# A two-layer diffusion backbone with expert retrieval: plain fp32 products while selecting, three-pass products only at the end

## The chip, the cores and the metric

The kernel runs on one core of a Trainium2 chip. The metric is the device time of one execution in microseconds; the median of three runs stands for a kernel. PE is TensorE, DVE is VectorE, ACT is ScalarE, POOL is GpSimd, SP the engine that issues most DMAs.

## What is computed

640 tokens (512 latent, 128 context) of width 1024 go through two layers. Each layer mixes tokens and then retrieves experts:

```python
def peer_ffn(h, wq, sub_keys, u_tab, v_tab):
    q = (x @ wq).reshape(n, PEER_HEADS, 2, PEER_DQ // 2)
    s = jnp.einsum('nhcd,hckd->nhck', q, sub_keys)
    s1, i1 = lax.top_k(s[:, :, 0], 16); s2, i2 = lax.top_k(s[:, :, 1], 16)
    cand = s1[..., :, None] + s2[..., None, :]
    top, pos = lax.top_k(cand, 16)          # per head, of 8 heads
    idx = take_along_axis(i1 * 128 + i2, pos); gate = softmax(top)
    act = gelu(einsum('nd,nhkd->nhk', x, u_tab[idx]))
    return einsum('nhk,nhkd->nd', gate * act, v_tab[idx])
```

`u_tab` and `v_tab` have 16384 rows of 1024 numbers in each layer.

## The kernel before

The program is written out engine by engine, with semaphores; no scheduler moves anything. A layer is a loop iteration (`nc.Fori(0, DEPTH)` in `build`) of stages; this case is about its second half.

Three of the five token tiles of 128 are computed densely: the hidden values of **all** 16384 experts are formed for the 384 tokens (ND), multiplied with a gate that is zero nearly everywhere, and multiplied with all of V. The other two tiles (SPARSE = 2) fetch only their own rows: 128 rows of U and 128 of V per token, gathered by POOL, one row for each of 128 tokens at a time.

U is treated in 128 blocks of 128 experts. A block is a load of 512 KB (`HiddenAhead.load`, on SP), a rounded high part (`u_high`, ACT, L1469), the low part that is left (`u_low`, DVE, L1473), and on PE eight times `split3`: low x high, high x low, high x high (L196 to L198) on fp32r operands, 384 columns each, into a PSUM bank. ACT then takes the GELU (L1491). Raw blocks, high and low parts each have two slots. The first 64 blocks (AHEAD) are done in the stages before the experts and stored to DRAM (`spill`):

- **Query** (`gemm(g, "query", ...)`): the second normalization (`norm_programs`) writes h as a high and a low part, g.h2; then the queries.
- **Selection** (`select_stage`): for each of five tiles, PE forms 16 score matrices (L1569, plain fp32, 128 x 128), DVE finds the top 16 of each, combines and selects (L1633 to L1717), ACT takes an exponent (L1617), PE turns the result (L1578). Blocks 0 to 51 of U are placed by hand between these steps: `PER_TILE = 11` blocks to a tile, with positions p at which PE turns the last tile's result (p == 1) and forms the next scores (p == 3), and at which ACT takes the exponent (p == 5); `low(t, p)` places the low parts in DVE's list.
- **Gates** (`gates_stage`): 12 turns with two half-tiles each. DVE makes one-hot matrices (L1782, L1783, L1788), PE multiplies them (L1805, 48 bf16 matmuls), half a U block follows on PE, ACT copies the gates out (L1831), SP stores them. Blocks 52 to 63.
- **Experts** (`experts_stage`): 32 turns. A turn takes four blocks of V (high part L1997, low part L2042), two spilled and two new hidden blocks, and weighs them with the gates (L2051, L2056). Between these steps DVE handles 16 gathered rows: in turns 0 to 15 a dot product of a U row with h of the token (L2065), tile 0 first and then tile 1; in turns 16 to 31 a multiply-add of a V row to the token's sum (L2074), again tile by tile, so that each row adds to the sum that the row before it wrote:

```python
r = gathered(i, q)
ve.wait_ge(used, i * PER_TURN + q)
ve.scalar_tensor_tensor(acc[:, x, :], r, w, acc[:, x, :], ALU.mult, ALU.add).then_inc(used, 1)
```

  The rows lie in a ring of 8 slots that POOL fills (L1912). At the start PE turns h of the two tiles into token order (L1965), after the gates have been stored (`stores_done`).

The order of work is set by these lists alone. SP's list holds loads and spills in order; POOL's holds the gathers.

Of the kernel before, what the change touches and what calls it, by code (L numbers as in the profile page):

```python
# [434 lines left out]
def norm_programs(g, st, name, out, gain, shift, low=None):  # L435
# [6 lines left out]
    sq = g.sb(st, "sq", [P, 2, NT])  # L442
    rs = g.sb(st, "rs", [P, 2, NT])
    t = g.sb(st, "t", [P, 3, NT])
    raw = (lambda kc: out[:, kc, :]) if low is None else (lambda kc: t[:, kc % 3, :])
# [30 lines left out]
    def vector(ve):  # L476
# [9 lines left out]
        for kc in range(KC):  # L486
            if low is not None and kc >= 3:
# [947 lines left out]
PER_TILE = 11  # L1435
IN_SELECT = 52
SPARSE = 2
# [4 lines left out]
class HiddenAhead:  # L1442
# [5 lines left out]

    def __init__(self, g, st, l):
        self.g, self.l = g, l  # L1450
        self.u = g.sb(st, "u", [P, 2, KC, P])
        self.u2 = [g.sb(st, f"u{x}", [P, 2, KC, P], F32R) for x in ("hi", "lo")]
        self.hh = g.sb(st, "hh", [P, 2, ND])
        self.u_in = [g.sem(f"u_loaded{i}") for i in range(2)]
        self.spilled = [g.sem(f"hidden_stored{i}") for i in range(2)]
        self.u_hi, self.u_lo, self.h_ready, self.h_taken = (g.sem(f"exp_{x}") for x in ("u_high", "u_low", "h_ready", "h_taken"))
# [7 lines left out]
    def u_high(self, act, n, slot, times, first=False):  # L1464

        act.wait_ge(self.u_in[slot], times * 16)
        if not first:
            act.wait_ge(self.h_ready, n - 1)
        self.g.nc.scalar.activation(self.u2[0][:, slot, :, :], self.u[:, slot, :, :], ACT.Copy).then_inc(self.u_hi, 1)  # L1469

    def u_low(self, ve, n, slot):
        ve.wait_ge(self.u_hi, n + 1)
        ve.tensor_tensor(self.u2[1][:, slot, :, :], self.u[:, slot, :, :], self.u2[0][:, slot, :, :].bitcast(F32),  # L1473
                         ALU.subtract).then_inc(self.u_lo, 1)

    def products(self, pe, slot, chunks):
# [6 lines left out]
    def hidden(self, pe, n, slot, first=False):  # L1483
        pe.wait_ge(self.u_lo, n + 1)
        if not first:
            pe.wait_ge(self.h_taken, n - 1)
        self.products(pe, slot, range(KC)).then_inc(self.h_ready, 1)
# [16 lines left out]
class Gathered:  # L1504
# [4 lines left out]
    def __init__(self, g, st):  # L1509
        self.rows = [g.sb(st, "rows", [P, P], U32) for _ in range(SPARSE)]  # L1510
        self.share = [g.sb(st, "share", [P, P]) for _ in range(SPARSE)]
        self.act = [g.sb(st, "act", [P, P]) for _ in range(SPARSE)]

    def row_numbers(self, ve, k, x, first, second, base):

        k.then(ve.scalar_tensor_tensor(self.act[x][:, :], first, float(NKEY), second, ALU.mult, ALU.add))
        k.did(ve.tensor_scalar(self.rows[x][:, :], self.act[x][:, :], base, None, ALU.add))


def select_stage(g, l, qT, sel, kt, loaded, hid, own):  # L1520
# [10 lines left out]
    lists = g.sem("sel_lists_done")  # L1531
    NC = 2 * PH
    TAIL = P - TOPK // 2
    with ExitStack() as st, nc.Block() as block:
# [17 lines left out]
        def blocks(t):  # L1552
            return [(n - t * PER_TILE, n) for n in range(t * PER_TILE, min((t + 1) * PER_TILE, IN_SELECT))]

        @block.sync
        def _(sync):
            for n in range(IN_SELECT):
                hid.load(sync, n + 2, n % 2)
# [3 lines left out]
        def _(pe):  # L1562
# [17 lines left out]

            pe.wait_ge(loaded, 16)
# [11 lines left out]
        def _(act):  # L1593
# [10 lines left out]
            hid.u_high(act, 0, 0, 1, first=True)  # L1604
            hid.u_high(act, 1, 1, 1, first=True)
            scores(0)
            for t in range(TILES):
                for p, n in blocks(t):
                    hid.u_high(act, n + 2, n % 2, n // 2 + 2)
                    hid.gelu_to_spill(act, n, n % 2, n // 2, first=n < 2)  # L1610
                    if p == 1 and t >= 1:
                        selected(t - 1)
                    if p == 3 and t + 1 < TILES:
                        scores(t + 1)
                    if p == 5:
# [5 lines left out]
        def _(ve):  # L1621
            k = Counter(ve, steps)

            def low(t, p):

                for q, n in blocks(t):
                    if q == p:
                        hid.u_low(ve, n + 2, n % 2)

            def top16(n, values, scratch, best, index, t, replaced, found):  # L1630
# [4 lines left out]
                for i in range(n):  # L1635
                    k.did(ve.match_replace(scratch[:, i, :], best[:, i, 0:8], values[:, i, :], NEG))
                    k.did(ve.max_index(index[:, i, 0:8], best[:, i, 0:8], values[:, i, :]))
                    if i in replaced:
                        low(t, replaced[i])
# [4 lines left out]
                for i in range(n):  # L1644
                    k.did(ve.max_index(index[:, i, 8:16], best[:, i, 8:16], scratch[:, i, :]))
                    if i in found:
                        low(t, found[i])
                k.wait()

            hid.u_low(ve, 0, 0)  # L1650
            hid.u_low(ve, 1, 1)
# [3 lines left out]
            for t in range(TILES):  # L1655
                ve.wait_ge(sc_taken, t + 1)
                top16(NC, s, s2, v16, i16, t, {3: 0, 13: 1}, {3: 2})
# [12 lines left out]
                low(t, 3)  # L1670
                k.wait()
                top16(PH, cand, c2, top, pos, t, {5: 4}, {})
                low(t, 5)
# [24 lines left out]
                low(t, 6)  # L1698
# [4 lines left out]

# [3 lines left out]
                for c in range(2):  # L1707
                    k.did(ve.tensor_reduce(res[:, c, :, :], oh[:, c, :, :, :].rearrange("p m k h -> p h k m"), AX.X, ALU.add))
                    if c == 0:
                        low(t, 7)  # L1710
# [7 lines left out]
                low(t, 8)  # L1718
                low(t, 9)
                low(t, 10)  # L1720
# [12 lines left out]
def gates_stage(g, l, sel, hid, store, own):  # L1733
# [8 lines left out]
    with ExitStack() as st, nc.Block() as block:  # L1742
# [9 lines left out]
        def turns(eng, body):  # L1752

            with eng.Fori(0, TG // 2 - 1) as i:
                for q in range(2):
# [642 lines left out]
```

## Time and profile before

| | |
|---|---|
| median of 3 runs | 5162.43 us (5157.72 to 5165.9) |
| profiled execution | 5158.91 us, its span 5157.1 us |
| PE busy | 4192.3 us, 81%; mean granted clock 0.891 |
| DVE busy | 3765.5 us, 73% |
| ACT busy | 1603.1 us, 31% |
| POOL busy | 1497.4 us, 29% |
| DMA | 1079 MB, 209 GB/s over the span |
| selection, gates, experts of layer 0 | 1072 to 1395, to 1560, to 2574 us |

A busy share is an average over stages with different limits. What counts is read stage by stage: which engine is full there, and what the others wait for. Starts of successive instructions tell what one really takes from its engine; the printed duration includes latency that overlaps the next one.

### The profile page before, as it was taken

How to read it: one execution, taken by the hardware profiler on the slowest of the kernel's cores; microseconds unless marked ns; L12 is line 12 of the kernel's file. 1: busy time of each engine (PE TensorE's matmuls, PEld its weight loads, DVE VectorE, ACT ScalarE, POOL GpSimd, SP SyncE). 2: the span in 40 equal slices, each digit the busy share in tenths (PEclk: the TensorE clock that was granted, in tenths of full speed). 3: DMA queues.
4: the chain of work that ended last, by engine and by line, in shares of the span. 5: the costliest groups of instructions: out<-in, count | busy, mean ns of one | idle time of the engine just before them, and what ended most of it. 6: DMA issues, size and time to landing. Idle time of an engine off the chain costs nothing. (4 is left out here: it accounts for less than half of the span.)

```text
span 5157.1 us, 78818 instructions
## 1 busy us (share of the span) xinstructions
PE 4192.3 (81%) x29134; PEld 3640.1 (71%) x29134; DVE 3765.5 (73%) x6707; ACT 1603.1 (31%) x2322; POOL 1497.4 (29%) x1046
## 2 busy tenths in 40 slices
PE   6975996888788888888778579869887788888886
PEld 4944775888777777777668257759876777777775
DVE  2245664369997999999932567533999799999997
ACT  3133542323242222222231435232333322222223
POOL 0000000000005777777600000000000076777774
PEclk8986987999998999999989779789999999999998
DMA  5140001223379999999921400011334799999996
GB/s 195 61 158 12 2 2 35 78 82 124 106 224 362 408 409 409 406 409 409 361 67 49 154 4 2 2 69 49 116 122 144 244 401 409 409 403 409 409 409 249
DMA packets 398567, 1079.12 MB, mean 209 GB/s; under 512 B 37248, under 2 KB 176768, under 8 KB 394752
## 3 DMA queue, kind: packets, MB, share of 16 engines
q1 hardware_dynamic: 250880, 539.10, 29.2%
q0 software_dynamic: 147456, 536.94, 26.3%
q8 instruction: 146, 2.39, 0.2%
q14 instruction: 85, 0.70, 0.0%
HBM read 996.47 MB, written 79.43 MB: 209 GB/s over the span
## 5 line engine op out<-in xcount | busy, mean ns | idle before, releaser
L1912 POOL DMA_INDIRECT ring<-peer_u_rows,rows x512 | 732.1, 1430 | 2756.7 <-issue 1333.4
L196 PE MATMUL ps<-vhi,wlo 128*128 128x512 f32 x1536 | 655.5, 427 | 276.0 <-DVE wlo L2056 275.4
L1912 POOL DMA_INDIRECT ring<-peer_v,rows x512 | 743.1, 1451 | 252.0 <-DVE acc L2074 166.1
L196 PE MATMUL ps<-hhi,ulo 128*128 128x384 f32 x2048 | 713.4, 348 | 102.1 <-DVE ulo L1473 97.8
L198 PE MATMUL ps<-hhi,uhi 128*128 128x384 f32 x2048 | 701.7, 343 | 0.0
L197 PE MATMUL ps<-hlo,uhi 128*128 128x384 f32 x2048 | 701.4, 342 | 0.0
L2074 DVE SCALAR_TENSOR_TENSOR acc<-ring,act,acc 128x1024 f32<-128x1024 f32 x512 | 660.1, 1289 | 23.1 <-DMA ring<-peer_v,rows 3.4
L2065 DVE SCALAR_TENSOR_TENSOR ring<-ring,acc 128x1024 f32<-128x1024 f32 x512 | 620.2, 1222 | 55.7 <-DMA ring<-peer_u_rows,rows 48.6
L197 PE MATMUL ps<-vlo,whi 128*128 128x512 f32 x1536 | 644.5, 420 | 0.0
L198 PE MATMUL ps<-vhi,whi 128*128 128x512 f32 x1536 | 640.8, 417 | 0.0
L196 PEld LDWEIGHTS ps<-vhi,wlo 128*128 128x128 f32 x1536 | 317.4, 207 | 369.5 <-issue 292.0
L196 PEld LDWEIGHTS ps<-hhi,ulo 128*128 128x128 f32 x2048 | 396.5, 194 | 127.0 <-DVE ulo L1473 119.2
L197 PEld LDWEIGHTS ps<-hlo,uhi 128*128 128x128 f32 x2048 | 396.4, 194 | 2.4
L198 PEld LDWEIGHTS ps<-hhi,uhi 128*128 128x128 f32 x2048 | 396.6, 194 | 0.0
L1469 ACT ACTIVATE uhi<-u 128x1024 fp32r<-128x1024 f32 x256 | 263.2, 1052 | 425.5 <-DMA u<-peer_u 346.3
L198 PEld LDWEIGHTS ps<-vhi,whi 128*128 128x128 f32 x1536 | 316.8, 206 | 72.6
L197 PEld LDWEIGHTS ps<-vlo,whi 128*128 128x128 f32 x1536 | 317.6, 207 | 67.4
L1473 DVE TENSOR_TENSOR ulo<-u,uhi 128x1024 fp32r<-128x1024 f32 x256 | 315.7, 1234 | 46.4 <-ACT uhi L1469 46.1
L2042 DVE TENSOR_TENSOR vlo<-v,vhi 128x1024 fp32r<-128x1024 f32 x256 | 312.9, 1222 | 26.8 <-ACT vhi L1997 26.3
L1997 ACT ACTIVATE vhi<-v 128x1024 fp32r<-128x1024 f32 x256 | 268.5, 1049 | 149.2 <-DMA v<-peer_v 149.2
L2002 ACT ACTIVATE whi<-ha 128x384 fp32r<-128x384 f32 x128 | 66.7, 522 | 757.0 <-DVE ha L2051 734.5
L196 PE MATMUL ps<-hhi,proj_lo 128*128 128x320 f32 x672 | 209.6, 312 | 22.4 <-DVE hlo L484 21.0
(333 smaller groups left out, 7844.2 us busy)
## 6 DMA issues: line engine op xcount, KB each, us to landing
u<-peer_u SPq DMA_DIRECT2D x256, 512.0 KB
v<-peer_v SPq DMA_DIRECT2D x256, 512.0 KB
gates<-stage SPq DMA_DIRECT2D x24, 2048.0 KB, 9.6
gw<-gates SPq DMA_DIRECT2D x64, 768.0 KB
mod_ring<-mod_late SPq DMA_DIRECT2D x16, 2048.0 KB, 8.8
hidden<-hh SPq DMA_DIRECT2D x128, 192.0 KB, 1.9
ha<-hidden SPq DMA_DIRECT2D x128, 192.0 KB
proj_raw<-w_proj SPq DMA_DIRECT2D x42, 512.0 KB, 3.6
```

Of the source, the lines that this page charges most:

```text
L196: pe.matmul(out, lhs[1], rhs[0], start=start, stop=False)
L197: pe.matmul(out, lhs[0], rhs[1], start=False, stop=False)
L198: return pe.matmul(out, lhs[0], rhs[0], start=False, stop=stop)
L1469: self.g.nc.scalar.activation(self.u2[0][:, slot, :, :], self.u[:, slot, :, :], ACT.Copy).then_inc(self.u_hi, 1)
L1473: ve.tensor_tensor(self.u2[1][:, slot, :, :], self.u[:, slot, :, :], self.u2[0][:, slot, :, :].bitcast(F32), ALU.subtract).then_inc(self.u ...
L1912: pool.indirect_dma_start(ring[:, m % RING, :], None, table, rows).then_inc(row_in[m % RING], 16)
L1997: nc.scalar.activation(v2[0][:, j, :], v[:, j % 2, :], ACT.Copy).then_inc(v_hi, 1)
L2002: nc.scalar.activation(w2[0][:, j, :], h, ACT.Copy).then_inc(w_hi, 1)
L2042: ve.tensor_tensor(v2[1][:, j, :], v[:, j % 2, :], v2[0][:, j, :].bitcast(F32), ALU.subtract).then_inc(v_lo, 1)
L2065: ve.scalar_tensor_tensor(r, r, 1.0, acc[:, x, :], ALU.mult, ALU.mult, accum_out=own.act[x][:, bass.ds((i - x * DOT_TURNS) * PER_TURN + q, ...
L2074: ve.scalar_tensor_tensor(acc[:, x, :], r, w, acc[:, x, :], ALU.mult, ALU.add).then_inc(used, 1)
```

## The change

1. In selection and gates a block of U is used as loaded: `products` issues 8 plain fp32 matmuls of the raw block and of raw h, in place of 24 on split operands. `u_high` and `u_low` are gone there. Raw blocks get four slots (`U_RING = 4`); a load waits for PE (`h_ready`) and no longer for DVE's low part.
2. The second normalization also keeps h raw (`kept`), and g.h2 is freed after the query product. Its scratch tiles lie in memory that is used later.
3. In selection each tile gets 10 or 11 blocks, all tiles evenly; the turned result comes at p == 3, scores at p == 6, the exponent at p == 8. h of the two sparse tiles is turned here (`tokens_first`, after the second and the fourth block).
4. Two long reduces (128 x 2048 to 128 x 128) are replaced by a tree of adds of 1024, 512, 256 and 128 elements.
5. The expert stage splits h (384 columns, both halves) and its U blocks itself (`x_high`, `x_low`, `u_high`, `u_low`). The spilled blocks' tile `ha` lies in the third slot of U.
6. The V rows of the two tiles alternate (`row_of`), except the first 16 and the last 16; a row waits for the last row of its own tile (`row_before`). The first row of a tile is a plain multiply, so the sums are not cleared. DVE's 32 turns are written out instead of looped; PER_TURN is still 16.

```diff
+U_RING = 4
     def load(self, sync, n, slot, first=False):
         if not first:
-            sync.wait_ge(self.u_lo, n - 1)
+            sync.wait_ge(self.h_ready, n - U_RING + 1)
...
     def products(self, pe, slot, bank, chunks):
         for kc in chunks:
-            mm = split3(pe, self.g.ps[:, slot, 0:ND], [x[:, slot, kc, :] for x in self.u2],
-                        [x[:, kc, 0:ND] for x in self.g.h2], start=(kc == 0), stop=(kc == KC - 1))
+            mm = pe.matmul(self.g.ps[:, bank, 0:ND], self.u[:, slot, kc, :], self.x[:, kc, 0:ND], start=(kc == 0), stop=(kc == KC - 1))
...
         def blocks(t):
-            return [(n - t * PER_TILE, n) for n in range(t * PER_TILE, min((t + 1) * PER_TILE, IN_SELECT))]
+            first = IN_SELECT * t // TILES
+            return [(n - first, n) for n in range(first, IN_SELECT * (t + 1) // TILES)]
...
             for t in range(TILES):
                 for p, n in blocks(t):
-                    hid.hidden(pe, n, n % 2, first=n < 2)
-                    if p == 1 and t >= 1:
+                    hid.hidden(pe, n, n // U_RING + 1, first=n < 2)
+                    if t == 0 and p in (1, 3):
+                        tokens_first(p // 2)
+                    if p == 3 and t >= 1:
                         turned(t - 1)
-                    if p == 3 and t + 1 < TILES:
+                    if p == 6 and t + 1 < TILES:
                         scores(t + 1)
...
+                for n in (TOPK // 2, TOPK // 4, TOPK // 8):
+                    for c in range(2):
+                        k.did(ve.tensor_tensor(oh[:, c, 0:n, :, :], oh[:, c, 0:n, :, :], oh[:, c, n:2 * n, :, :], ALU.add))
+                    k.wait()
...
-                for c in range(2):
-                    k.did(ve.tensor_reduce(res[:, c, :, :], oh[:, c, :, :, :].rearrange("p m k h -> p h k m"), AX.X, ALU.add))
...
                     ve.tensor_tensor(ob[:, o % 2, :, :, :], keys, col(1, o), ALU.is_equal).then_inc(b_ready, 1)
-                    if o == NO - 1:
-                        hid.u_low(ve, t + (N0 + 2), q)
...
+def row_of(m):
+    if m < DOTS:
+        return divmod(m, P)
+    m -= DOTS
+    if m < LEAD:
+        return 0, m
+    if m < 2 * P - LEAD:
+        half, x = divmod(m - LEAD, 2)
+        return x, half + LEAD * (1 - x)
+    return 1, m - P
...
+            def x_low(half):
+                kc = slice(half * KC // 2, (half + 1) * KC // 2)
+                ve.wait_ge(x_hi, half + 1)
+                ve.tensor_tensor(x2[1][:, kc, :], hid.x[:, kc, 0:ND], x2[0][:, kc, :].bitcast(F32), ALU.subtract).then_inc(x_lo, 1)
...
+                w, acc = own.act[x][:, slot:slot + 1], own.acc[:, x, :]
+                ve.wait_ge(used, row_before(m) + 1)
+                if slot == 0:
+                    ve.tensor_scalar(acc, r, w, None, ALU.mult).then_inc(used, 1)
+                else:
+                    ve.scalar_tensor_tensor(acc, r, w, acc, ALU.mult, ALU.add).then_inc(used, 1)
...
-            ve.memset(acc[:, :, :], 0.0).then_inc(shared, 1)
...
+            for i in range(NG):
+                turn(i, i == LAST)
```

PE at the start of selection, before (psum out, moving and stationary operand behind the arrow):

```order
L1569 MATMUL ps<-kt,qT 128x128 x16
L196 MATMUL ps<-hhi,ulo 128x384
L197 MATMUL ps<-hlo,uhi 128x384
L198 MATMUL ps<-hhi,uhi 128x384
L196 MATMUL ps<-hhi,ulo 128x384
```

and the same place now:

```order
L1565 MATMUL ps<-kt,qT 128x128 x16
L1464 MATMUL ps<-h,u 128x384 x16
L1582 MATMUL ps<-keep,h 128x128 x8
L1464 MATMUL ps<-h,u 128x384 x16
L1582 MATMUL ps<-keep,h 128x128 x8
L1464 MATMUL ps<-h,u 128x384 x24
L1565 MATMUL ps<-kt,qT 128x128 x16
L1464 MATMUL ps<-h,u 128x384 x56
L1574 MATMUL ps<-keep,res 128x128 x3
```

Eight matmuls make a block where there were 24; the next tile's scores come after seven blocks, and a tile's result is turned four blocks into the next tile.

DVE in the gates, one turn near the end of the stage, before:

```order
L1782 TENSOR_TENSOR ea<-iota_tokens,sel_123 128x2048
L1783 TENSOR_TENSOR ob<-iota_tokens,sel_123 128x2048
L1473 TENSOR_TENSOR ulo<-u,uhi 128x1024
L1788 TENSOR_TENSOR oa<-ea,sel_123 128x2048 x3
L1782 TENSOR_TENSOR ea<-iota_tokens,sel_123 128x2048
L1783 TENSOR_TENSOR ob<-iota_tokens,sel_123 128x2048
```

and now:

```order
L1773 TENSOR_TENSOR ea<-iota_tokens,sel_120 128x2048
L1774 TENSOR_TENSOR ob<-iota_tokens,sel_120 128x2048
L1777 TENSOR_TENSOR oa<-ea,sel_120 128x2048 x3
L1773 TENSOR_TENSOR ea<-iota_tokens,sel_120 128x2048
L1774 TENSOR_TENSOR ob<-iota_tokens,sel_120 128x2048
```

The low part between the one-hot matrices is gone; nothing else of DVE's list moves there.

## Rows read from the trace of the kernel before

**Rows 1.** the page's part on 40 slices: DVE's busy tenths, and GB/s moved by DMA

```profile
DVE  2245664369997999999932567533999799999997
...
GB/s 195 61 158 12 2 2 35 78 82 124 106 224 362 408 409 409 406 409 409 361 67 49 154 4 2 2 69 49 116 122 144 244 401 409 409 403 409 409 409 249
```

**Rows 2.** busy time by stretch: us, PE, PEld, DVE, ACT, POOL, clock, DMA, GB/s

```profile
1000.00:1050.00 50.00, 50.00 (x343) 50.00 (x342) 14.35 (x14) 7.42 (x7) 0.00 (x0) 1.00 0.17 53
1072.00:1395.00 323.00, 262.04 (x1423) 250.67 (x1423) 295.94 (x1142) 104.07 (x132) 0.00 (x0) 0.93 0.37 117
1395.00:1560.00 165.00, 128.88 (x1455) 121.22 (x1456) 153.36 (x138) 62.46 (x48) 0.00 (x0) 0.97 0.69 198
1560.00:2574.00 1014.00, 865.35 (x3891) 744.99 (x3889) 951.73 (x1217) 277.84 (x386) 738.35 (x512) 0.92 1.02 402
```

**Rows 3.** who waited for whom in selection: total us, times, longest

```profile
ACT uhi L1469 <- DMA u<-peer_u: 171.3, 41, 5.2
...
PE ps L196 <- DVE ulo L1473: 48.1, 34, 1.9
```

**Rows 4.** order of time on PE, end of selection: start, us, what, [idle before]

```profile
1393.37 0.90 PE L1578 MATMUL ps<-keep,res 128*128 128x128 f32 x3 [11.54 <-DVE res L1717]
1395.25 0.66 PE L196 MATMUL ps<-hhi,ulo 128*128 128x384 f32 x1 [0.98 <-PEq L1534]
```

**Rows 5.** order of time on DVE in the gates

```profile
1424.06 1.22 DVE L1782 TENSOR_TENSOR ea<-iota_tokens,sel 128x2048 bf16<-128x2048 bf16 x1
...
1429.74 1.23 DVE L1782 TENSOR_TENSOR ea<-iota_tokens,sel 128x2048 bf16<-128x2048 bf16 x1
...
1436.55 1.23 DVE L1782 TENSOR_TENSOR ea<-iota_tokens,sel 128x2048 bf16<-128x2048 bf16 x1
```

**Rows 6.** busy time of one expert turn with dot rows, one with value rows

```profile
1629.00:1660.00 31.00, 28.14 (x123) 24.12 (x122) 29.49 (x47) 8.69 (x13) 23.39 (x19) 0.89 1.03 408
2146.00:2177.00 31.00, 26.79 (x122) 23.17 (x121) 30.42 (x31) 8.66 (x12) 23.52 (x17) 0.94 1.03 408
```

**Rows 7.** DVE's first V low part of turns 0, 15, 16 and 31

```profile
1585.98 1.23 DVE L2042 TENSOR_TENSOR vlo<-v,vhi 128x1024 fp32r<-128x1024 f32 x1 [5.62 <-ACT vhi L1997]
...
2049.83 1.22 DVE L2042 TENSOR_TENSOR vlo<-v,vhi 128x1024 fp32r<-128x1024 f32 x1
...
2084.22 1.23 DVE L2042 TENSOR_TENSOR vlo<-v,vhi 128x1024 fp32r<-128x1024 f32 x1 [0.23 <-DVE acc L2135]
...
2548.52 1.22 DVE L2042 TENSOR_TENSOR vlo<-v,vhi 128x1024 fp32r<-128x1024 f32 x1
```

**Rows 8.** order of time on PE, start of selection

```profile
1072.63 3.81 PE L1569 MATMUL ps<-kt,qT 128*128 128x128 f32 x32 [1.19 <-PEq L215]
1076.20 0.42 PE L196 MATMUL ps<-hhi,ulo 128*128 128x384 f32 x1
1076.46 0.34 PE L197 MATMUL ps<-hlo,uhi 128*128 128x384 f32 x1
...
1081.84 0.33 PE L198 MATMUL ps<-hhi,uhi 128*128 128x384 f32 x1
```

**Rows 9.** plain fp32 matmuls elsewhere on PE: two pairs of 512 and 128; 32 rows

```profile
341.31 2.41 PE L725 MATMUL ps<-xconv,lruw 128*128 128x512 f32 x8
343.64 1.92 PE L340 MATMUL ps<-mod_ring,scond 128*32 128x512 f32 x16
...
643.18 0.92 PE L1152 MATMUL ps<-proj 32*128 32x384 f32 x4
643.93 0.39 PE L1154 MATMUL ps<-proj 32*128 32x128 f32 x4
```

**Rows 10.** order of time on PE, the first half-tile of the gates

```profile
1404.90 2.93 PE L1805 MATMUL ps<-ob,oa 128*128 128x128 bf16 x48 [3.12 <-DVE oa L1788]
1407.65 0.42 PE L196 MATMUL ps<-hhi,ulo 128*128 128x384 f32 x1
```

**Rows 11.** order of time on ACT, start of the expert stage

```profile
1564.65 1.02 ACT L2025 ACTIVATE acc<-ps 128x1024 f32<-128x1024 f32 x1 [9.12 <-DMA gates<-stage]
```

More of the change, by code:

```diff
@@ L432, in _, with norm_programs @@
             mod_shifts(g, Counter(ve, steps), g.modE[:, bass.ds(l * 2 * KC, 2 * KC), :], 0, 2 * KC, (0, "n1", 1))
-def norm_programs(g, st, name, out, gain, shift, low=None):
+def norm_programs(g, st, name, out, gain, shift, low=None, kept=None, scratch=None):
     nc = g.nc
@@ L486, in vector @@
         for kc in range(KC):
-            if low is not None and kc >= 3:
+            if low is not None and kept is None and kc >= 3:
                 ve.wait_ge(lowed, kc - 2)
@@ L1434 @@
 AHEAD = 64
-PER_TILE = 11
 IN_SELECT = 52
+U_RING = 4
 SPARSE = 2
@@ L1531, in select_stage @@
     lists = g.sem("sel_lists_done")
+    turned_h, tok_ready = (g.sem(f"ahead_{x}") for x in ("h_turned", "h_ready"))
     NC = 2 * PH
@@ L1622, in _, with top16 @@
             k = Counter(ve, steps)
[L1624 to L1630, printed above, removed]
+            def top16(n, values, scratch, best, index):
                 for i in range(n):
@@ L1894, in stores_done @@
                 eng.wait_ge(hid.spilled[q], 16 * (AHEAD // 2))
-        def turns(eng, turn):
-            with eng.Fori(0, LAST) as i:
-                turn(i, False)
-            turn(LAST, True)
         @block.gpsimd
@@ L1993, in _, with x_high, u_high @@
         def _(act):
+            def x_high(half):
+                kc = slice(half * KC // 2, (half + 1) * KC // 2)
+                nc.scalar.activation(x2[0][:, kc, :], hid.x[:, kc, 0:ND], ACT.Copy).then_inc(x_hi, 1)
+            def u_high(i, b, first=False):
+                act.wait_ge(hid.u_in[b], i * 16 + 16 * (AHEAD // U_RING + 1))
+                if not first:
+                    act.wait_ge(hid.h_ready, i * 2 + (AHEAD + b - 1))
+                nc.scalar.activation(u2[0][:, b, :, :], hid.u[:, b, :, :], ACT.Copy).then_inc(u_hi, 1)
             def v_high(i, j):
@@ L2019, in gelu_own @@
                 nc.scalar.activation(own.act[x][:, :], own.act[x][:, :], ACT.Gelu).then_inc(acted, 1)
+            x_high(0)
+            u_high(0, 0, first=True)
+            x_high(1)
+            u_high(0, 1, first=True)
             stores_done(act)
             act.sem_inc(added, GB)
-            for x in range(SPARSE):
-                act.wait_ge(turned_h, x + 1)
-                nc.scalar.activation(acc[:, x, :], g.flat[:, 1024 * (x + 1):1024 * (x + 2)], ACT.Copy).then_inc(tok_ready, 1)
             for j in range(2):
@@ L2069, in value, with weights_of @@
-            def value(x):
-                def row(i, q):
-                    r = gathered(i, q)
-                    ve.wait_ge(used, i * PER_TURN + q)
-                    w = own.act[x][:, bass.ds((i - (SPARSE + x) * DOT_TURNS) * PER_TURN + q, 1)]
-                    ve.scalar_tensor_tensor(acc[:, x, :], r, w, acc[:, x, :], ALU.mult, ALU.add).then_inc(used, 1)
-                return row
-            def turn(i, last, row):
-                def rows(*which):
-                    for q in which:
-                        row(i, q)
+            def weights_of(x):
+                ve.wait_ge(acted, x + 1)
+                ve.tensor_tensor(own.act[x][:, :], own.act[x][:, :], own.share[x][:, :], ALU.mult).then_inc(shared, 1)
+                ve.wait_ge(shared, x + 1)
@@ new lines, in row @@
+            def row(m):
+                x, slot = row_of(m)
+                r = ring[:, m % RING, :]
+                if m >= DOTS and slot == 0:
+                    weights_of(x)
+                ve.wait_ge(row_in[m % RING], 16 * (m // RING + 1))
+                if m < DOTS:
+                    own.dot(ve, r, x, slot).then_inc(used, 1)
+                    return
+                w, acc = own.act[x][:, slot:slot + 1], own.acc[:, x, :]
[4 more added lines that the diff above has]
+                    ve.scalar_tensor_tensor(acc, r, w, acc, ALU.mult, ALU.add).then_inc(used, 1)
@@ L2082, in turn, with rows @@
+            def turn(i, last):
+                at = iter(range(i * PER_TURN, (i + 1) * PER_TURN))
+                def rows(n):
+                    for _ in range(n):
+                        row(next(at))
                 v_low(i, 2)
-                rows(0, 1)
+                rows(2)
                 weigh(i, 2)
-                rows(2)
+                rows(1)
                 w_low(i, 2)
                 v_low(i, 3)
-                rows(3)
+                rows(1)
                 weigh(i, 3)
-                rows(4)
+                rows(1)
```

271 lines of the change are left out of this document (125 added, 146 removed).

## The prediction

> **What bounds the kernel now.** I read the page's 40 slices first, then the busy time by stage, then the waits and the order of time inside each stage. The slices say where VectorE (DVE) and the DMA engines are full [rows 1]: DVE reads 9 in most slices of selection, gates and experts, and the DMA rate stands near 409 GB/s only in the expert stage. The stages of the first layer are selection 1072 to 1395 us, gates to 1560 and experts to 2574 [rows 2]; the second layer repeats them. Each has its own limit.
>
> *Selection*: DVE is busy 296 of 323 us and TensorE (PE) 262, so neither is full. The two hand each other work. A block of U is split into high and low parts, and only two slots exist. PE waited 48.1 us, in 34 pieces, for the low part, while ACT's split waited 171.3 us for the block to arrive [rows 3]. So the stage runs on a ring: load, high part, low part, products. PE then idles 11.54 us at the end, for the last tile's DVE work [rows 4].
>
> *Gates*: DVE is busy 153 of 165 us [rows 2], and half-tiles follow each other without a gap on DVE, 5.68 us without a low part and 6.81 us with one [rows 5]. DVE is the bound.
>
> *Experts*: both DVE (952 of 1014 us) and the DMA (402 GB/s, share 1.02) are near full [rows 2]. A turn with dot rows and one with value rows move the same 408 GB/s; DVE is busy 29.49 of 31 us in the first, 30.42 in the second [rows 6]. Dot turns last (2049.83 - 1585.98)/15 = 30.92 us, value turns (2548.52 - 2084.22)/15 = 30.95 us [rows 7]. As the dot turns have DVE time to spare and are no shorter, the bytes set the pace.
>
> **Part 1: plain fp32 in selection.** It removes 24 one-pass matmuls of 384 columns a block. From 1076.46 to 1081.84 there are 31 steps [rows 8]: 0.1735 us each, 24 x 0.1735 = 4.16 us a block. In their place stand 8 plain matmuls. What does one cost at 384 columns? The score matmuls are plain fp32, 128 by 128: two records each, 16 of them in 1076.20 - 1072.63 = 3.57 us [rows 8], 0.223 us each; by columns, 384 make 0.669 us. The gate matmuls of the recurrence, plain, take 2.33 us for two pairs of 512 + 128 columns, 1280 in all, at full clock [rows 9]: 0.70 us for 384. If only columns grow and the small remainder stays (128 columns at four clocks of 2.4 GHz are 0.213 us, so 0.010 is left), it is 0.65 us. The only 384-column plain matmuls, on 32 rows, come two in 0.75 us [rows 9]; should these not have run beside each other that is 0.375 us, and if they ran side by side up to 0.75. The lower reading is excluded as a price here by the 128-row rows. I keep 0.65 to 0.75 and take 0.669, from the row with the same rows and weights of 128 by 128: 5.36 us a block, **1.20 us more PE time than now**.
>
> The Trainium skill ("FP8 and Floating Point Precision", TensorE Precision Notes) says that true fp32 takes four passes through the array, which speaks against this change, since the split form takes three. By it alone, with no remainder, a block would be an estimated 5.12 us and the two layers another 25 us faster than my sum; the score row agrees with four passes and shows a remainder on top.
>
> What goes for it: no low part on DVE, 52 x 1.13 = 59 us of its 296, and no high part on ACT. The tree of adds in place of two long reduces comes on top; I cost it at nothing, as DVE at 296 - 59 = 237 us lies beside about 300 us of PE. Its cover is PE: with a tile about 60 us long, DVE has 12 us to spare. The longer add chain and the wait for the exponent, now issued after the ninth block of a tile, stay within that, and the transposes of a tile come four blocks into the next. Behind the exponent's wait on ACT stand the GELUs of the last blocks, on which PE's banks depend; DVE is then long past the differences. The copy of a block now waits for PE two blocks back and has three blocks (16 us) to land, against a longest wait of 5.2 us today [rows 3], so SP's queue of loads and spills costs nothing.
>
> Selection then is PE's own work: 52 x 5.36 = 278.7; five score groups 5 x 3.57 = 17.9; five groups of transposes at 0.90 [rows 4], 4.5; the token transposes moved here, 16 at no more than 0.30, I take half, 2.4. Sum 303.5 us, against 1395.25 - 1072.63 - 0.98 of stage change = 321.6 us. **Minus 18.1 us a layer.** With PE never waiting I take full clock: 1000 to 1050 us, with PE busy all of it, has a granted clock of 1.00; selection now has 0.93 [rows 2]. At 0.65 it is minus 26.4, at 0.70 minus 5.7, at 0.75 plus 15.2.
>
> **Part 2: gates.** DVE loses 12 low parts of 1.13 us: **minus 13.6 us a layer**. PE must still fit beneath 5.68 us a half-tile: 48 one-hot matmuls 1407.65 - 1404.90 = 2.75 us [rows 10], 4 x 0.669 = 2.68, about 0.1 for the change: 5.53. It fits by 0.15 us, at 0.70 just so (5.65). DVE is next in line and stays the bound.
>
> **Part 3: experts.** Splitting h and the first two U blocks here is four copies on ACT and four subtractions on DVE, some 6 us; they lie beside the gate store, for which ACT waits 9.1 us before the stage can load anything [rows 11], so they cost nothing. Without that cover they would cost 6 us. PE loses 32 transposes that lie there too. Bytes are unchanged, so turns stay at 30.92 us. DVE is released in value turns (alternate tiles have no chain, save the first and last 16 rows), by at most 30.42 - 29.49 = 0.9 us a turn, and then waits for rows instead: nothing. What goes is the stop between the kinds of row, 34.39 us for turn 15 [rows 7]. So 31 turns take 31 x 30.92 = 958.6 instead of 962.5: **minus 3.9 us**. The last turn keeps its chain. Written-out turns instead of a loop: bounds by the same rows, 0 to a gain that the DMA hides. The normalization's own rows, without the ring of three, and the two earlier prefetches of U: nothing, ACT paces the one and PE's first blocks are far off.
>
> **Sum.** 18.1 + 13.6 + 3.9 = 35.6 us a layer, 71.2 us in two. The profiled execution takes 5158.91 us (span 5157.1), which gives 5087.7; the median of the runs lies 3.5 us above it, so 5162.4 - 71.2 = **5091 us**. With 0.65 and 0.70 us a matmul: 5074 and 5116. That is the forecast's own range.
>
> **Rivals.**
> - *The matmul is dearer, 0.70 to 0.75 us.* PE then takes back what DVE gives. At 0.75 selection is 15.2 longer, gates are 24 x (6.25 - 5.85) = 9.6 shorter (5.85 is PE's half-tile), experts 3.9 shorter: plus 1.7 a layer, 5166 us, no change. For: the 32-row row [rows 9]. Against: both 128-row rows. From 0.70 to 0.74: 12%; no change: 6%.
> - *The clock turns it slower.* If PE keeps being granted less than full clock although it never waits, every pass stretches and PE is now the bound. At 0.89, as the turn at 1629 us has [rows 6], a block takes 6.02 us, selection 52 x 6.02 + 27.8 = 340.9 (plus 19.3), gates gain 1.1, experts 3.9: plus 14.3 a layer, **5191 us**. It decides from a mean clock of about 0.92 down (selection 5.83 us a block). For: the lower clocks in every stage but one. Against: each of these stages has PE idling, and the full stretch shows 1.00. 6%.
> - *The expert stage gains too.* If the DMA can go faster once DVE stops holding slots, value turns fall to DVE's own work, 29.49 us: (30.95 - 29.49) x 15 = 21.9 us a layer, 5091 - 43.8 = 5047 us. Against: dot turns, which have that slack already, move 408 GB/s and no more. 8%. The Trainium skill ("DMA: Bandwidth & Descriptors", Where 436 GB/s comes from) puts the ceiling at 435 GB/s, and by it there would be room for this; no stretch here exceeds 409.
> - *The change doesn't free DVE*: a wait that I overlooked, such as the exponent, could keep tiles at 64 us. Then the gates' gain alone is left, 5128 us; in the 12% above.
>
> **How the numbers follow.** Forecast 68%, dearer matmul 12%, no change 6%, slower 6%, experts too 8%. A measurement can tell about 0.2%, 10 us. Faster: 68 + 12 + 8 = 88%; same 6%; slower 6%. The range 5058 to 5140 takes in both ends of the forecast, most of the dearer case and the near part of the last rival, and leaves out some 18%.
>
> **What would show it.** Right: two records a matmul in selection at about 0.33 us a step, no PE wait there above 1 us, granted clock near 1.00, DVE idle some 70 us of 303; gates half-tiles at 5.68 us on DVE; the same 409 GB/s in all turns, with DVE waiting on rows of V now as it does on rows of U. Wrong: a step of 0.35 us or more, a clock under 0.95 in selection, PE gaps where transposes or scores stand, or value turns under 30 us.

## The result, and the profile after

The changed kernel takes **5079.02 us** (median of 4 runs, 5077.3 to 5083.16) against 5164.16 us before (4 runs): ratio 0.9836, 95% interval 0.9824 to 0.9848, so 85 us faster. Forecast were 5091 us and a range of 5058 to 5140. The profiled execution has a span of 5076.1 us (before 5157.1), 81.0 us less, and the first layer accounts for half of that. One execution among the experiments, at 5273 us with a granted clock of 0.785, is left out of the numbers below. The forecast beside each stretch is the prediction's term:

| stretch of layer 0, us | before | after | measured | forecast |
|---|---|---|---|---|
| selection, first score to first block of the gates | 322.6 | 291.1 | -31.5 | -18.1 |
| gates, from there to the start of the stage's last copy | 158.4 | 143.2 | -15.2 | -13.6 |
| from there to the first low part of V in turn 0 | 32.3 | 30.5 | -1.8 | 0 |
| 31 expert turns | 962.5 | 969.2 | **+6.7** | -3.9 |
| the stages ahead, which start selection later | | | +1.4 | 0 |

The first three stretches moved as forecast or further; the expert turns went the wrong way. In the second layer selection falls from 325.9 to 291.1 us. Busy time by stage, as in [rows 2] (selection, gates, experts; columns us, PE, PEld, DVE, ACT, POOL, clock, DMA share, GB/s):

```profile
1073.00:1365.00 292.00, 289.82 (x1023) 179.03 (x1023) 215.53 (x1119) 54.50 (x80) 0.00 (x0) 1.00 0.45 127
1365.00:1530.00 165.00, 144.68 (x1392) 112.74 (x1392) 147.65 (x133) 56.82 (x42) 7.80 (x8) 0.95 0.77 226
1530.00:2534.00 1004.00, 847.88 (x3793) 729.89 (x3794) 943.86 (x1213) 274.55 (x384) 705.45 (x505) 0.92 1.01 401
```

In selection PE is now busy for 289.8 of 292 us at a granted clock of 1.00, the level of 2.4 GHz, where it had 0.93 with waits in it. DVE fell from 296 to 216 us. The order of time on PE in selection, which answers to [rows 4] and [rows 8]:

```profile
1073.99 3.81 PE L1565 MATMUL ps<-kt,qT 128*128 128x128 f32 x32 [1.18 <-PEq L215]
1077.64 4.68 PE L1464 MATMUL ps<-h,u 128*128 128x384 f32 x14
...
1119.09 36.29 PE L1464 MATMUL ps<-h,u 128*128 128x384 f32 x112
1155.21 0.49 PE L1574 MATMUL ps<-keep,res 128*128 128x128 f32 x3
1155.54 4.68 PE L1464 MATMUL ps<-h,u 128*128 128x384 f32 x14
...
1363.33 0.49 PE L1574 MATMUL ps<-keep,res 128*128 128x128 f32 x3
1365.07 5.40 PE L1464 MATMUL ps<-h,u 128*128 128x384 f32 x16 [1.25 <-PEq L1529]
```

Seven blocks are 112 records in a row, two a matmul, in 1155.21 - 1119.09 = 36.12 us: 0.3225 us a record, **0.645 us a matmul, 5.16 us a block**. The transposes of a tile cost 1155.54 - 1155.21 = 0.33 us among other work, and the 11.54 us idle ahead of the last ones are gone. Who waited in selection [rows 3]:

```profile
ACT hh L1475 <- PE ps L1464: 204.0, 47, 4.7
DVE sm L1703 <- ACT res L1623: 58.9, 5, 17.5
```

PE itself waits for no other engine's work: the others wait for it, DVE for the exponent, which sits behind GELUs that wait for products. In the gates DVE's half-tiles [rows 5] are all of one length, 1397.29 - 1391.61 = 5.68 us (PE is behind DVE at first and follows at its own 5.39 us for eight half-tiles, until it has caught up):

```profile
1391.61 1.21 DVE L1773 TENSOR_TENSOR ea<-iota_tokens,sel 128x2048 bf16<-128x2048 bf16 x1
...
1397.29 1.22 DVE L1773 TENSOR_TENSOR ea<-iota_tokens,sel 128x2048 bf16<-128x2048 bf16 x1
...
1402.96 1.21 DVE L1773 TENSOR_TENSOR ea<-iota_tokens,sel 128x2048 bf16<-128x2048 bf16 x1
```

The first low parts of V in turns 0, 15, 16 and 31, as in [rows 7]:

```profile
1538.79 1.23 DVE L2067 TENSOR_TENSOR vlo<-v,vhi 128x1024 fp32r<-128x1024 f32 x1 [5.60 <-ACT vhi L2011]
...
2006.32 1.22 DVE L2067 TENSOR_TENSOR vlo<-v,vhi 128x1024 fp32r<-128x1024 f32 x1
...
2037.52 1.22 DVE L2067 TENSOR_TENSOR vlo<-v,vhi 128x1024 fp32r<-128x1024 f32 x1
...
2508.00 1.21 DVE L2067 TENSOR_TENSOR vlo<-v,vhi 128x1024 fp32r<-128x1024 f32 x1
```

Dot turns last (2006.32 - 1538.79)/15 = 31.17 us (30.92 before), value turns (2508.00 - 2037.52)/15 = 31.37 (30.95), and turn 15 has lost its stop: 31.20 instead of 34.39. Seen one by one, the turns are not all longer. Most last 30.7 to 31.5 us, and eight of the 31 last 32.05 to 32.43. One more line differs, the queue of instruction fetches in the DMA view (packets, MB, share of 16 engines), over these 31 turns. After:

```profile
q14 instruction: 16, 0.13, 0.0%
```

and before:

```profile
q14 instruction: 6, 0.05, 0.0%
```

Each of the eight long turns has one of the 16 fetches in it; the other eight fetches stand in turns of 31.50 us or less. (A second queue of instruction packets, q8, has 1 packet here and 2 before.)

### The profile page after: what moved, and what is told of

It reads as the page before. It is cut to its first block and busy times, and to the rows that moved or that the text cites. A ratio compares the mean times of both kernels' runs of the same rounds, so it can differ in the third digit from the quotient of the medians.

```text
span 5076.1 us, 74252 instructions
## 1 busy us (share of the span) xinstructions
PE 4257.7 (84%) x28014; PEld 3460.9 (68%) x28014; DVE 3577.3 (70%) x6641; ACT 1486.5 (29%) x2198; POOL 1446.1 (28%) x1046
## 5 line engine op out<-in xcount | busy, mean ns | idle before, releaser
L1507 POOL DMA_INDIRECT ring<-peer_v,rows x512 | 709.9, 1387 | 291.0 <-DVE acc L2102 209.8
L1464 PE MATMUL ps<-h,u 128*128 128x384 f32 x2048 | 674.8, 488 | 2.5 <-PEq L1529 2.5
L1464 PEld LDWEIGHTS ps<-h,u 128*128 128x128 f32 x2048 | 384.3, 190 | 256.6 <-issue 3.5
L196 PE MATMUL ps<-xhi,ulo 128*128 128x384 f32 x1024 | 344.2, 336 | 18.6 <-DVE xlo L2059 18.6
L198 PE MATMUL ps<-xhi,uhi 128*128 128x384 f32 x1024 | 344.1, 336 | 0.0
L197 PE MATMUL ps<-xlo,uhi 128*128 128x384 f32 x1024 | 343.6, 336 | 0.0
L2016 ACT ACTIVATE whi<-u 128x384 fp32r<-128x384 f32 x128 | 66.7, 522 | 784.4 <-DVE u L2076 784.4
L1475 ACT ACTIVATE hh<-ps 128x384 f32<-128x384 f32 x256 | 122.9, 480 | 437.3 <-PE ps L1464 437.1
L2016 ACT ACTIVATE whi<-hh 128x384 fp32r<-128x384 f32 x128 | 67.4, 526 | 508.7 <-DVE hh L2076 493.3
L197 PE MATMUL ps<-hlo,proj_hi 128*128 128x320 f32 x672 | 209.0, 311 | 0.0
```

The source lines that it names most:

```text
L196: pe.matmul(out, lhs[1], rhs[0], start=start, stop=False)
L197: pe.matmul(out, lhs[0], rhs[1], start=False, stop=False)
L198: return pe.matmul(out, lhs[0], rhs[0], start=False, stop=stop)
L1464: mm = pe.matmul(self.g.ps[:, bank, 0:ND], self.u[:, slot, kc, :], self.x[:, kc, 0:ND], start=(kc == 0), stop=(kc == KC - 1))
L1475: return self.g.nc.scalar.activation(self.hh[:, slot, :], self.g.ps[:, slot, 0:ND], ACT.Gelu)
L1507: return pool.indirect_dma_start(to, None, table, rows)
```

## Experiments

The theory for selection (P): PE alone sets it now. For the gates: DVE sets them. For the expert stage two theories stood against each other: A, the written-out DVE turns cost time through instruction fetches; B, alternating rows and a faster DVE upset the order of the loads.

**Selection: the long reduces back.** The edit in the changed kernel:

```diff
-                for n in (TOPK // 2, TOPK // 4, TOPK // 8):
-                    for c in range(2):
-                        k.did(ve.tensor_tensor(oh[:, c, 0:n, :, :], ..., ALU.add))
-                    k.wait()
-                ... (the last add, into res)
+                for c in range(2):
+                    k.did(ve.tensor_reduce(res[:, c, :, :], oh[:, c, :, :, :].rearrange("p m k h -> p h k m"), AX.X, ALU.add))
```

> The changed kernel with the two long reduces of a tile (3.79 us each) back in place of the tree of adds (1.61 us for each index), ahead of the wait for the exponent. Theory P, TensorE alone sets the length of selection: VectorE's extra 4.35 us a tile lie in its waits for the exponent (58.9 us in 5), selection stays at 291 us, the kernel at 5079 give or take 3. Rival, VectorE's chain still sets part of a tile: selection grows by up to 21.8 us a layer, 5122.

Measured: 5079.0 us (5 runs, 5076.79 to 5082.28), ratio to before 0.9836 (0.9823 to 0.9849): no change. DVE's wait for the exponent shrank by what the reduces add:

```profile
DVE sm L1698 <- ACT res L1623: 38.9, 5, 13.5
```

10 reduces of 3.7 us stand in place of 16.1 us of adds, 21 us more, and 58.9 - 38.9 = 20.0 us of wait took them in. The tree of adds is worth nothing in this kernel; theory P holds.

**Selection: a quarter of the products.**

```diff
-        self.products(pe, n % U_RING, n % 2, range(KC)).then_inc(self.h_ready, 1)
+        self.products(pe, n % U_RING, n % 2, (0, KC - 1)).then_inc(self.h_ready, 1)
```

> The changed kernel, which in selection multiplies two of the eight chunks of each U block only (six of eight products are left out, so the hidden values are others). TensorE's work there falls from 289 to about 88 us a layer. Theory P, TensorE alone sets selection in the change: what is left is VectorE's work, 5 tiles of 43 us, so selection takes about 225 us instead of 291 and the kernel about 4947 us. Rival, the chain of GELU and exponent on ScalarE or the loads would hold tiles anyway: selection stays above 260 us, the kernel above 5015. Gates are to stay at 143 us (5.68 us a half-tile on VectorE) under both.

Measured: 4945.76 us (4 runs, 4942.98 to 4949.25), 133 us under the change, 66.6 a layer. The end of selection on PE:

```profile
1295.03 0.90 PE L1574 MATMUL ps<-keep,res 128*128 128x128 f32 x3 [28.39 <-DVE res L1711]
1296.92 2.90 PE L1464 MATMUL ps<-h,u 128*128 128x384 f32 x4 [0.99 <-PEq L1529]
```

With the first score at 1072.14, selection takes 224.8 us and now ends on DVE, for which PE stands 28.4 us. So in the change PE bounds selection and DVE has some 66 us to spare. The gates' copies into the stage stay 5.66 us apart, (1441.5 - 1311.3)/23.

**Gates: the low part's work back.**

```diff
+                    if o == NO - 1:
+                        ve.tensor_tensor(again[:, :], own.acc[:, 0, :], own.acc[:, 1, :], ALU.subtract)
```

> The changed kernel with one more VectorE subtraction of 128 x 1024 in each tile of the gate stage (1.13 us, into a buffer that nobody reads), that is, the low part's work put back there without its waits. If VectorE sets the gate stage, as the sum had it, the twelve of them cost their full time: 143.2 us become 156.8, and the kernel 5079 + 27 = 5106 us. If TensorE, 5.38 us busy of each 5.68, or the loads set it now, part of it is hidden: at most 24 x (5.68 - 5.38) = 7 us a layer can be, so down to 5092.

Measured: 5110.38 us (4 runs, 5107.43 to 5111.48), 31.4 more than the change. The copies into the stage span 1521.9 - 1377.8 = 144.1 us where they spanned 128.2: 15.9 a layer. On DVE the half-tile with the extra operation lasts 1429.08 - 1422.27 = 6.81 us, exactly as in the kernel before:

```profile
1422.27 1.23 DVE L1774 TENSOR_TENSOR ea<-iota_tokens,sel 128x2048 bf16<-128x2048 bf16 x1
...
1424.54 1.24 DVE L1777 TENSOR_TENSOR again<-acc 128x1024 fp32r<-128x1024 f32 x1
...
1429.08 1.24 DVE L1774 TENSOR_TENSOR ea<-iota_tokens,sel 128x2048 bf16<-128x2048 bf16 x1
```

DVE sets the gates; nothing of the 13.6 us was hidden. The 2.3 us beyond it stand at the very end, in the last 48 one-hot products on PE. In this run, in the change and in the kernel before they are:

```profile
1516.67 5.18 PE L1797 MATMUL ps<-ob,oa 128*128 128x128 bf16 x48 [3.89 <-DVE oa L1780]
...
1505.29 2.93 PE L1794 MATMUL ps<-ob,oa 128*128 128x128 bf16 x48 [2.75 <-DVE oa L1777]
...
1549.11 4.50 PE L1805 MATMUL ps<-ob,oa 128*128 128x128 bf16 x48 [3.89 <-DVE oa L1788]
```

The granted clock over them is 0.52, 1.00 and 0.62. With the longer half-tiles PE stands idle longer ahead of them, and the same work takes 5.18 - 2.93 = 2.25 us more than in the change. Why the clock falls there was not tested.

**Experts: loops in the change.** The turns of DVE are looped again, with the slot of a row worked out from the loop's counter (`dots`, `values`; their bodies are left out here, and three turns stay written out):

```diff
-            for i in range(NG):
-                turn(i, i == LAST)
+            per = P // PER_TURN
+            with ve.Fori(0, per) as i:
+                turn(i, False, dots(0))
+            with ve.Fori(per, 2 * per) as i:
+                turn(i, False, dots(1))
+            for i in (2 * per, 2 * per + 1):
+                turn(i, False, fixed)
+            with ve.Fori(2 * per + 2, LAST) as i:
+                turn(i, False, values)
+            turn(LAST, True, fixed)
```

> The changed kernel, with VectorE's expert turns as loops again (turns 0 to 7, 8 to 15 and 18 to 30; turns 16, 17 and 31 stay written out); order of rows and everything else as in the change. Theory A, the written-out turns cost time (their instructions have to be fetched through DMA engines that are already full: 17 packets of instruction fetch in the expert stage against 9 before): dot turns go from 31.17 back to 30.92 us and value turns from 31.37 to 30.95, 31 turns from 969.2 to about 959, the kernel from 5079 to about 5058. Theory B, the alternation of value rows and the faster VectorE rows upset the loads: nothing changes, dot turns 31.2, value turns 31.4, 5079.

Measured: **5062.89 us** (5 runs, 5048.53 to 5066.71), ratio to before 0.9797 (0.9783 to 0.9812), 16 us under the change. The 31 turns take 961.8 us, dot turns 30.93. Value turns are at 31.12, not 30.95; that part of A's number missed, and the part on the prediction says why. The fetches over the 31 turns:

```profile
q14 instruction: 7, 0.06, 0.0%
```

**Experts: tile by tile, still written out.** One constant: `LEAD = P` in place of `LEAD = 16`, which makes the value rows of tile 0 come first and those of tile 1 after them.

> The changed kernel, written out as it is, but with the value rows of one tile after the other, so every value row waits for the one before it. Theory A (written-out instructions): value turns stay at 31.4 us, the kernel at 5079 give or take 5; the rows are chained again at 2.67 us a pair. Theory B (alternation): value turns go back to 30.95 us, 15 turns x 0.42 x 2 layers = 12.6 us less, 5066.

Measured: 5080.68 us (5 runs, 5060.81 to 5083.65): as the change. Its 31 turns take 970.8 us, value turns 31.47, with 16 fetches. B falls: without the alternation the loss is still there.

**Experts: the kernel before, written out.** Its four loops over turns become `for i in range(...)`, nothing else.

> The kernel before, with one thing changed: VectorE's expert turns written out instead of looped. Theory A: its dot turns grow from 30.92 to about 31.17 us and its value turns to about 31.3, so 31 turns grow by some 9 us and the kernel by 18, to 5182. Theory B: no change, 5164.

Measured: 5182.84 us (5 runs, 5181.34 to 5185.32), ratio to before 1.0036 (1.0023 to 1.0050): 17 us slower by that edit alone. Its 31 turns grow from 962.5 to 969.9 us (second layer 963.4 to 971.6), and the fetches from 6 to 16.

**Experts: more instructions, and the control.** The changed kernel, and the looped version, with

```diff
+                        for _ in range(3):
+                            ve.wait_ge(x_lo, 2)
```

ahead of each row.

> The changed kernel with three more waits of VectorE ahead of every gathered row, all long satisfied (48 in a turn, about as many instructions as a turn had). If fetching instructions is what written-out turns cost, the fetches in the expert stage rise from 17 to about 28 a layer, more turns are long ones, and at 0.9 us a fetch the kernel goes from 5079 to about 5100. If it is not the fetch but something else about the written-out turns (registers, branches, their order), the time stays at 5079.

> The control for the same extra waits: the version with looped turns (5062.9 us) with the same three waits ahead of every row. If the waits themselves cost nothing, since VectorE passes them while a row is computed, it stays at 5063 and at 8 fetches in the expert stage; if they cost time by themselves, it grows by as much as the written-out version does.

Measured: written out 5092.1 us (5 runs, 5087.94 to 5095.02), 13 more than the change; 31 turns take 976.0 us, and 15 of them are over 31.7. The fetches rose to 23, not to the 28 I had reckoned. In the loop the same waits give 5065.6 us (5 runs, 5052.52 to 5069.72; ratio to before 0.9816, 0.9797 to 0.9835), 963.2 us for 31 turns and 8 fetches: within the scatter of 5062.9. Waits that are already met cost DVE nothing; fetching them does.

How a fetch shows in a turn: DVE's order of time in the change, in turn 24 (it starts at 2289.58, has a fetch at 2307.1 and lasts 32.43 us):

```profile
2307.95 1.27 DVE L2102 SCALAR_TENSOR_TENSOR acc<-ring,act,acc 128x1024 f32<-128x1024 f32 x1
2310.35 1.29 DVE L2102 SCALAR_TENSOR_TENSOR acc<-ring,act,acc 128x1024 f32<-128x1024 f32 x1 [1.14 <-DMA ring<-peer_v,rows]
2311.57 1.21 DVE L2067 TENSOR_TENSOR vlo<-v,vhi 128x1024 fp32r<-128x1024 f32 x1
2312.90 1.28 DVE L2102 SCALAR_TENSOR_TENSOR acc<-ring,act,acc 128x1024 f32<-128x1024 f32 x1
2315.35 1.28 DVE L2102 SCALAR_TENSOR_TENSOR acc<-ring,act,acc 128x1024 f32<-128x1024 f32 x1 [1.16 <-DMA ring<-peer_v,rows]
```

and the same place of turn 25 (from 2322.01, no fetch, 30.66 us), in which no row is waited for until 23.4 us into the turn:

```profile
2340.38 2.47 DVE L2102 SCALAR_TENSOR_TENSOR acc<-ring,act,acc 128x1024 f32<-128x1024 f32 x2
2342.77 1.21 DVE L2067 TENSOR_TENSOR vlo<-v,vhi 128x1024 fp32r<-128x1024 f32 x1
2343.90 1.27 DVE L2102 SCALAR_TENSOR_TENSOR acc<-ring,act,acc 128x1024 f32<-128x1024 f32 x1
2345.39 1.28 DVE L2102 SCALAR_TENSOR_TENSOR acc<-ring,act,acc 128x1024 f32<-128x1024 f32 x1 [0.22 <-DMA ring<-peer_v,rows]
```

DVE never stands for an instruction ("issue"). It stands for a row that lands late: in seven of the eight long turns for 1.14 to 1.34 us, 20.8 to 21.6 us into the turn, where rows arrive just in time; in turn 16 the waits are spread over 23 to 27 us. The turn after is shorter (30.66), so not all of the 1.3 us is lost.

**Experts: fetches by another engine.** Does it matter who fetches? First the looped version with ScalarE's turns written out (`for i in range(...)` in place of its three loops):

> The version with looped VectorE turns (5062.9 us), but with ScalarE's expert turns written out. ScalarE is busy 269 of 962 us there and has idle time in each turn. Theory M, the fetch costs by what it does to the full DMA engines, whoever asks for it: some 6 more fetches a layer cost about 0.9 us each, 5063 goes to about 5074, with turns of 32 us or more again. Theory S, only the engine that sets the turn loses, as it stands still for its own instructions: no change, 5063.

Measured: 5065.03 us (5 runs, 5062.21 to 5070.79), 962.2 us for 31 turns with 11 fetches against 7. In the first layer turns 4, 11 and 25, with ScalarE's added fetches, last 31.10, 30.95 and 31.09 us, which spoke for S. In the second layer the same turns last 31.07, 31.72 and 32.07 us, so even here the last of them shows a cost. Then the same with many more instructions on ScalarE:

```diff
             def w_high(i, j):
+                for _ in range(24):
+                    act.wait_ge(x_hi, 2)
                 act.wait_ge(weighed, i * GB + (j + 1))
```

> The version with looped VectorE turns and ScalarE's turns written out (5065.0 us, 11 fetches in the expert stage), with 24 more waits of ScalarE, all long satisfied, ahead of its wait for each weighed block, where it stands idle 4 to 6 us: 96 more instructions a turn, some 23 more fetches a layer. Theory M (a fetch costs by what it does to the DMA engines, whoever asks): 23 x 0.9 us x 2 layers = 41 us more, 5106. Theory S (only VectorE's own fetches cost): 5065, turns of 31.1 us with a fetch in most of them. If ScalarE's waits themselves hold it up, turns grow evenly, with and without a fetch.

> The control for the run with ScalarE's fetches (5074.3 us, 23 fetches a layer in the expert stage, turns that alternate between 32.1 and 30.7 us): the same 24 waits ahead of each of ScalarE's four weighed copies of a turn, but in a loop, so that they are fetched once. If the fetches made the long turns there, this one has 8 to 10 fetches, even turns of 31.1 us and 5063 to 5065. If the waits themselves, which hold ScalarE up, made them, the turns alternate here too and the kernel takes 5074.

Measured: written out 5074.28 us (5 runs, 5060.1 to 5085.38), 31 turns 970.1 and 968.5 us in the two layers, with

```profile
q14 instruction: 23, 0.19, 0.0%
```

The control with the same waits in a loop: 5063.7 us (5 runs, 5059.42 to 5069.12), 961.9 and 961.5 us, with

```profile
q14 instruction: 9, 0.07, 0.0%
```

Written out, turns alternate between about 32 and 30.7 us from turn 16 on, the long ones being those with ScalarE's fetch, and show the same late row (turn 26, from 2337.04):

```profile
2358.02 1.28 DVE L2123 SCALAR_TENSOR_TENSOR acc<-ring,act,acc 128x1024 f32<-128x1024 f32 x1 [1.28 <-DMA ring<-peer_v,rows]
```

In the control they are 31.1 us each from turn 20 on. So a fetch by an engine that has time to spare costs too (theory M), through the rows that VectorE waits for. I had reckoned with 23 more fetches at 0.9 us and 5106 us, and got 14 against the control at about half that price; the times of the runs overlap (5060 to 5085 against 5059 to 5069), and it is the turns of both layers that show the cost. Why most of the added fetches of the run before it cost nothing visible, nor those at 6 us into turns 14 and 22, which the looped kernels have too, stays open.

| 31 turns, two layers | fetches a layer | us a layer | us a fetch |
|---|---|---|---|
| before, written out against looped | 16 against 6 | 969.9, 971.6 against 962.5, 963.4 | 0.8 |
| the change, written out against looped | 16 against 7 | 969.2, 969.2 against 961.8, 961.6 | 0.8 |
| the change, more waits, against without | 23, 22 against 16 | 976.0, 975.4 against 969.2, 969.2 | 1.0 |
| ScalarE written out with waits, against looped | 23 against 9 | 970.1, 968.5 against 961.9, 961.5 | 0.5 |

**Experts: loops, tile by tile.** The looped version with `LEAD = P` and two loops for the value turns, one for each tile:

> The version with looped VectorE turns (5062.9 us), with the value rows of one tile after the other instead of alternating, so each row waits for the one before it (2.67 us a pair instead of 2.5). If the bytes set the turn and VectorE's time does not matter, nothing changes: 5063. If the alternation is worth VectorE's time in value turns, they grow, by up to 30.42 - 29.49 = 0.9 us each and 28 us in all, 5091. If on the other hand the faster rows are what makes value turns 31.1 us here against 30.95 in the kernel before, they shrink and the kernel takes 5058.

Measured: 5064.96 us (5 runs, 5049.86 to 5070.33), ratio to before 0.9796 (0.9781 to 0.9811): the same as 5062.9. Value turns are 31.11 us against 31.12. The alternation is worth at most 1.4 us a layer (963.2 against 961.8), within the scatter of the runs; the bytes set the turn, and value turns of 31.1 us are not its doing.

## Why the prediction was right, and where it was not

**What bounds each stage**: right in all three. Selection was a ring between PE and DVE and is PE's own work now (both selection runs); the gates are DVE's (the run with the low part's work back); the expert stage is the DMA's.

**Part 1, selection, -18.1 forecast, -31.5 measured.** The mechanism held, and the size of one term was off: the plain matmul of 384 columns, taken as 0.669 us by scaling the score row whole, costs 0.645. The end "if only columns grow and the small remainder stays" (0.65) was the right reading; 52 blocks times 8 times 0.024 are 10.0 us. The transposes, taken at 0.90 a tile from a row after an idle stretch, cost 0.33 (2.9 us for five), and the token transposes 1.8 instead of 2.4. Together 13.5, the whole of the difference. No run has the plain products with the old places of blocks and transposes, so how the 31.5 us divide between the two is not shown. The prediction gave a block by the four passes alone as an estimated 5.12 us (the Trainium skill, "FP8 and Floating Point Precision", TensorE Precision Notes). Measured are 5.16, so that rule alone would have been nearer than my scaling. What I costed at nothing was nothing: the tree of adds, the wait for the exponent, the queue of loads.

**The rivals on PE.** With PE never waiting the granted clock is 1.00 over selection, so the clock did not turn it slower, and at 0.645 us the matmul was not dearer than taken. DVE was freed; the 5128 us given for the rival in which it is not count the expert term too, the gates alone would give 5135.

**Part 2, gates, -13.6 forecast, -15.2 measured.** Right: 13.6 us are DVE's, and PE's half-tile of 5.385 us fits beneath 5.68. The 1.6 us more are the last one-hot products, which take 2.93 us at full clock where they took 4.50 at 0.62. The prediction had no term for that.

**Part 3, experts, -3.9 forecast, +6.7 measured: the sign was wrong, and two steps failed.** The first is the sentence on written-out turns, bounded "0 to a gain that the DMA hides". I had let go of the loss side without a reason that excludes it. The loss was there: +7.4 a layer, the difference of 969.2 and 961.8. The page of the profile lists instruction packets, and the prediction does not weigh them. The second is "31 x 30.92", which books the stop of turn 15 as 3.4 us to be gained. Without it and with loops, 31 turns take 961.8 us, 0.8 less than before (961.6 and 1.8 less in the second layer). The stop was one of DVE, not of the DMA, as the stretch of that turn before shows:

```profile
2049.83:2084.22 34.39, 29.53 (x130) 25.26 (x129) 31.43 (x51) 9.00 (x13) 23.73 (x17) 0.87 1.03 408
```

408 GB/s during the stop: the loads ran on, and the turns behind it were shorter. Turns 16 to 20 lasted 30.72 to 30.76 us, those from 22 to 29 then 31.09 to 31.13, as turns 20 to 29 of the looped change (31.07 to 31.10). So 30.95 was a mean of both, and 30.92 one that holds turn 0 with 28.90; the pace of the bytes is 31.1 us in both kinds of turn, and 28.9 + 30 x 31.1 = 961.9 us meets the 961.8 of the looped change. The prediction itself says "the bytes set the pace"; followed to its end, a stop of an engine that isn't the bound gives nothing. Splitting h beside the gate store cost nothing, as forecast. The rival in which the expert stage also gains did not come: no stretch with loops moves over 409 GB/s.

**The sum**: 35.6 us a layer forecast, 40.5 measured. The total came close because the gains in selection, 13.4 us more than forecast, and in the gates and behind them, 3.4 more, outweighed an error of 10.6 the other way and 1.4 in the stages ahead. That is luck. The faster kernel is the change with DVE's loops kept: 5062.9 us, 2.0% under the kernel before.

## What to carry to other kernels

Where the DMA engines are full, written-out code is not free: count the extra instructions, look at the queue of instruction fetches on the profile's page, and loop any stage that lives on the DMA; here 9 or 10 fetches a layer cost about 8 us. A stop of an engine that is not the bound is no gain to book, and the test is whether the bound resource paused with it. Plain fp32 against split operands is decided by what the splitting costs the other engines: here a block takes 5.16 us of PE in place of 4.16, and DVE's work in selection fell by 59 us with the low parts (the other 21 of its 80 are the tree of adds, which bought nothing).

## What the runs showed of the hardware

- An instruction fetch is one packet of about 8 KB (0.13 MB in 16), 0.34 us of one of the 16 DMA engines (2.1% of their time over the microsecond at 2307), and yet the 31 turns lose 0.5 to 1.0 us for each. The late row is mostly 1.14 to 1.34 us late, about what a 512 KB load takes at 408 GB/s (1.28 us), as if it came one transfer later in line. That is an estimate from sizes; no run tells the order of the transfers.
- The Trainium skill ("Runtime: NRT & Kernel Launch", Instruction fetch mechanics) calls the cost of a refill mostly hidden. Selection agrees: 13 such fetches at a DMA share of 0.45, and PE is busy 60.00 of 60 us in its inner stretches. Beside a saturated DMA the runs disagree, with 16 to 17 us for 18 to 20 more fetches in two layers.
- Plain fp32 runs at 0.3225 us a record of 384 columns in a stretch of 112 records, 2.5 ns over 2 x 384 columns at 2.4 GHz; the score group's records of 128 columns are about 5 ns over theirs, so the remainder does not grow with the columns.
- The granted clock over the last 48 one-hot products of the gates is 1.00 in the change, where PE stood idle 2.75 us before them, and 0.52 and 0.62 in the run with the low part's work back and in the kernel before, where PE stood idle 3.89 us before them and also between the half-tiles. The same 48 products took 2.93, 5.18 and 4.50 us.
- The scatter of 15 to 20 us in some kernels' runs (5048.5 to 5066.7 with loops) lies, in the three traces that show it, in the stages ahead of selection. The first score of layer 0 stands at 1056 us in the tile-by-tile version and in the one with ScalarE's fetches, at 1070 to 1077 in the others; both have a granted clock of 0.83 over 400 to 600 us, the change 0.76. In the third, the loop with more waits, the short stretch is that ahead of the second layer's selection.
